# Gate and up of the FFN by seven half-size products for 19 of 22 feature tiles (Strassen's scheme) in a one-core DiT step

## The reference

```
def swiglu(h, wg, wu, wd):
    return (jax.nn.silu(h @ wg) * (h @ wu)) @ wd

xs = xs + gt2 * swiglu(modulate(rmsnorm(xs, g_ffn), sh2, sc2), w_gate, w_up, w_down)   # latent
xp = xp + ...                                                                          # context, the same
```

## Time and profile before

| | us |
|---|---|
| median of 3 runs | 970.76 (970.47, 970.76, 974.79) |
| the profiled execution | 974.25 |
| its span, first to last instruction | 972.3 |
| TensorE busy | 952.2 |
| VectorE busy | 492.9 |
| ScalarE busy | 356.7 |

### The profile page before, as it was taken

One profiled execution on the slowest core, in us unless ns is written; L12 is line 12 of the kernel. 1 busy time (PEld: TensorE's weight loads), 2 busy tenths in 40 slices (PEclk: granted clock), 3 DMA queues, 4 the chain that ended last, 5 costly groups with the idle time before them and its releaser, 6 DMA issues.

```text
span 972.3 us, 16382 instructions
## 1 busy us (share of the span) xinstructions
PE 952.2 (98%) x6613; PEld 894.5 (92%) x6613; DVE 492.9 (51%) x898; ACT 356.7 (37%) x675; POOL 2.8 (0%) x8
## 2 busy tenths in 40 slices
PE   5999999999999999999999999999999999999998
PEld 5688888778878999999999999999999999999998
DVE  4557898798788553233476233242323323333332
ACT  4563454667766422222257232211222221122220
POOL 0000000000000000000000000000000000000000
PEclk7899999999999999999999999999999999999999
DMA  9745333532353122422122212122222213122221
GB/s 373 297 176 185 138 109 131 178 111 88 125 162 128 63 68 80 181 71 72 53 68 86 87 65 85 45 97 78 67 84 65 86 44 109 65 85 67 68 81 68
DMA packets 33066, 104.23 MB, mean 107 GB/s; under 512 B 3696, under 2 KB 8944, under 8 KB 31856
## 3 DMA queue, kind: packets, MB, share of 16 engines
q1 hardware_dynamic: 32288, 102.64, 30.6%
q10 hardware_dynamic: 720, 0.77, 0.2%
HBM read 99.07 MB, written 4.33 MB: 106 GB/s over the span
## 4 chain that ended last, share of the span: by engine, by line
PE 91%; DVE 4%; DMA 1%; ACT 1%; SPq 1%; issue 1%; ACTq 0%; DVEq 0%
PE ps L1280 65%; PE ps L1376 13%; PE ps L1584 4%; PE ps L1502 3%; PE ps L1476 2%; PE ps L1487 2%; PE ps L1329 1%; PE ps L1400 1%; DMA x<-w_ada 1%; DVE scr L922 1%; DMA vec<-vecs 1%; SPq L466 1%; ACT scr L547 0%; DVE scr L1073 0%; DVE w_lo L886 0%
## 5 line engine op out<-in xcount | busy, mean ns | idle before, releaser
L535 ACT ACTIVATE w_hi<-stage 128x1024 fp32r<-128x1024 f32 x118 | 124.5, 1060 | 312.1 <-PE ps L1280 269.3
L886 DVE TENSOR_TENSOR w_lo<-stage,w_hi 128x1024 fp32r<-128x1024 f32 x118 | 144.4, 1224 | 173.7 <-ACT w_hi L535 170.7
L1280 PE MATMUL ps<-h_hi,w_hi 128*128 128x320 f32 x896 | 208.5, 314 | 0.7 <-ACT scr L709 0.4
L1280 PE MATMUL ps<-h_lo,w_hi 128*128 128x320 f32 x896 | 204.1, 309 | 0.0
L1280 PE MATMUL ps<-h_hi,w_lo 128*128 128x320 f32 x896 | 204.0, 309 | 0.0
L1280 PEld LDWEIGHTS ps<-h_hi,w_hi 128*128 128x128 f32 x896 | 148.2, 188 | 10.9 <-issue 9.0
L1280 PEld LDWEIGHTS ps<-h_lo,w_hi 128*128 128x128 f32 x896 | 149.8, 188 | 0.0
L1280 PEld LDWEIGHTS ps<-h_hi,w_lo 128*128 128x128 f32 x896 | 149.8, 188 | 0.0
L1280 PE MATMUL ps<-y_hi,w_hi 128*128 128x320 f32 x480 | 109.4, 309 | 0.0
L1280 PE MATMUL ps<-y_hi,w_lo 128*128 128x320 f32 x480 | 109.3, 309 | 0.0
L1280 PE MATMUL ps<-y_lo,w_hi 128*128 128x320 f32 x480 | 109.3, 309 | 0.0
(11 more groups left out here) (166 smaller groups left out, 1162.6 us busy)
## 6 DMA issues: line engine op xcount, KB each, us to landing
stage<-w_main SPq DMA_DIRECT2D x118, 512.0 KB, 3.5
x<-w_ada SPq DMA_DIRECT2D x23, 512.0 KB, 4.7
qk<-w_ada SPq DMA_DIRECT2D x7, 1024.0 KB, 11.7
bb<-rpb SPq DMA_DIRECT2D x16, 256.0 KB, 4.4
qk<-w_ada SPq DMA_DIRECT2D x5, 512.0 KB, 3.9
x<-x_t SPq DMA_DIRECT2D x1, 2560.0 KB, 11.0
y_t<-x SPq DMA_DIRECT2D x8, 320.0 KB, 2.2
vf<-w_ada SPq DMA_DIRECT2D x4, 512.0 KB, 3.9
```

The costliest lines, as they stand in the source:

```text
L535: act.activation(w_hi[:, slot, :], stage[:, slot, :], ACT.Copy).then_inc(hi_done, 1)
L886: dve.tensor_tensor(w_lo[:, slot, :], stage[:, slot, :], w_hi[:, slot, :].bitcast(F32), ALU.subtract).then_inc(lo_done, 1)
L1280: ins = pe.matmul(out[:, half, :], wt[:, w_slot, w], rt[:, rk, half * TH:(half + 1) * TH], start=start and n == 0, stop=stop and n == 2)
```

## The change

The diff, cut to its core (semaphores, aliases and the calls of the head left out):

```diff
+N_STD = 3
+LEFT = ("A11", "A12", "S2", "S1", "S3", "S4", "A22")
+LEFT_AT = {"A11": (0, 0), "A12": (0, 512), "S2": (1, 0), "S1": (1, 512), "S3": (2, 0), "S4": (2, 512), "A22": (3, 0)}
+BANK_OF = {"A11": 0, "A12": 1, "S2": 2, "S1": 3, "S3": 4, "A22": 5, "S4": 6}
...
+        def unit_used(u):
+            for part, nf in enumerate(FF_PARTS):
+                for n in range(KT):
+                    if u == down_unit(part, n):
+                        return lo_done, split_number(part, n) + 1
+                for f in range(max(FF_FIRST[part], N_STD), FF_FIRST[part] + nf):
+                    if u == gate_unit(f):
+                        return left_lo["S4"], f - N_STD + 1
+                    if u == gate_unit(f) + 1:
+                        return left_lo["A22"], f - N_STD + 1
+            return lo_done, u + 1
...
+            for u in range(U_WO, N_UNITS):
+                sp.wait_ge(*unit_used(u - RING))
+                load_unit(u, u % RING)
...
+                for f in range(max(FF_FIRST[part], N_STD), FF_FIRST[part] + nf):     # ScalarE
+                    g, more = f - N_STD, f + 1 < FF_FIRST[part] + nf
+                    prev = f > max(FF_FIRST[part], N_STD)
+                    left_high("A22", g)
+                    if prev:
+                        half_tanh(g - 1, 1)
+                    copy_p1(g)
+                    if more:
+                        left_high("A11", g + 1)
+                    else:
+                        split_down(part, 0)
+                    if prev or f == N_STD:
+                        a_high(f - 1)
+                    if more:
+                        left_high("A12", g + 1)
+                    half_tanh(g, 0)
+                    if more:
+                        for op in ("S1", "S2", "S3", "S4"):
+                            left_high(op, g + 1)
+                    else:
+                        split_down(part, 1)
+                        half_tanh(g, 1)
+                        a_high(f)
...
+            def c11_u2(g):                                                            # VectorE
+                dve.wait_ge(left_used["S2"], g + 1)
+                dve.wait_ge(p1_copied, g + 1)
+                dve.tensor_tensor(two(H_C11, H_U2), of_product("A12", "S2"),
+                                  by_half[:, H_P1:H_P1 + 1, :].to_broadcast([P, 2, TH]), ALU.add).then_inc(c11_done, 1)
...
+                    if prev:
+                        c21_c12(g - 1)
+                    elif f == N_STD:
+                        gated_up(f - 1)
+                    left_low("A22", g)
+                    if prev:
+                        products_gated(g - 1)
+                    if more:
+                        left_low("A11", g + 1)
+                        s3(g + 1)
+                    else:
+                        down_low(part, 0)
+                    if prev or f == N_STD:
+                        a_low(f - 1)
+                    c11_u2(g)
+                    if more:
+                        left_low("A12", g + 1)
+                        s1(g + 1)
+                    v_sum(g)
+                    if more:
+                        s2(g + 1)
+                        s4(g + 1)
+                    else:
+                        down_low(part, 1)
+                    c22_u3(g)
+                    if more:
+                        for op in ("S1", "S2", "S3", "S4"):
+                            left_low(op, g + 1)
+                    else:
+                        c21_c12(g)
+                        products_gated(g)
+                        a_low(f)
...
+            def product(op, g):                                                       # TensorE
+                pe.wait_ge(left_lo[op], g + 1)
+                if g == 0 and op not in ("A11", "A12", "S4"):
+                    pe.wait_ge(t_ready, ("S1", "S2", "S3", "A22").index(op) + 1)
+                slot, at = LEFT_AT[op]
+                for k in range(4):
+                    w = slice(at + k * P, at + (k + 1) * P)
+                    for n, (wt, part) in enumerate(((w_hi, 0), (w_hi, 1), (w_lo, 0))):
+                        ins = pe.matmul(ps[:, BANK_OF[op], 0:TH], wt[:, slot, w], right(op, part, k),
+                                        start=k == 0 and n == 0, stop=k == 3 and n == 2)
+                ins.then_inc(left_used[op], 1)
...
+                        free = [(p1_copied, g), (c11_done, g), (v_done, g), (c22_done, g), (c12_done, g)]
+                    pe.wait_ge(*free[0])
+                    product("A11", g)
+                    pe.wait_ge(*free[1])
+                    product("A12", g)
+                    product("S2", g)
+                    pe.wait_ge(*free[2])
+                    product("S1", g)
+                    pe.wait_ge(*free[3])
+                    product("S3", g)
+                    pe.wait_ge(*free[4])
+                    product("S4", g)
+                    product("A22", g)
```

More of the change, by code:

```diff
@@ new lines, in gate_tanh, with a_high, t_high @@
+            def gate_tanh(f):
+                act.wait_ge(pe_unit, U_FFN + 2 * f + 1)
+                act.activation(halves(ft[f % 2]), slot_ps(2 * (f % 2)), ACT.Tanh, scale=0.5).then_inc(tanh_done, 1)
+            def a_high(f):
+                act.wait_ge(a32_done, f + 1)
+                part = sum(f >= first for first in FF_FIRST) - 1
+                act.activation(y_hi[:, f - FF_FIRST[part], :], fp[f % 2], ACT.Copy).then_inc(ahi_done, 1)
+            def t_high(i):
+                act.wait_ge(t_sum, i + 1)
+                full = (t1_sb[:, :, :], t2_sb[:, :, :], b1[:, :, TH:T], b2[:, :, 0:TH])[i]
+                act.activation(t_hi[:, 4 * i:4 * i + 4, :], full, ACT.Copy).then_inc(t_hi_done, 1)
@@ new lines, in split_down @@
+            def split_down(part, n):
+                u = down_unit(part, n)
+                last = FF_FIRST[part] + FF_PARTS[part] - N_STD
+                act.wait_ge(*unit_arrived(u))
+                if n < 4:
+                    act.wait_ge(left_used[("A12", "S1", "S4", "A22")[n]], last)
+                else:
+                    act.wait_ge(pe_unit, split_number(part, n - 4) + 1)
+                act.activation(w_hi[:, n % 4, :], stage[:, u % RING, :], ACT.Copy).then_inc(hi_done, 1)
+            gate_tanh(0)
@@ new lines, in down_low @@
+            def down_low(part, n):
+                number = split_number(part, n)
+                dve.wait_ge(hi_done, number + 1)
+                slot = n % 4
+                dve.tensor_tensor(w_lo[:, slot, :], stage[:, down_unit(part, n) % RING, :], w_hi[:, slot, :].bitcast(F32),
+                                  ALU.subtract).then_inc(lo_done, 1)
+            t_sums(0)
+            gated(0)
+            split_lo(U_FFN + 4, (U_FFN + 4) % RING)
+            gated_up(0)
+            split_lo(U_FFN + 5, (U_FFN + 5) % RING)
@@ L1613, in _ @@
                         rms2_stats(1)
-            for part, nf in enumerate(FF_PARTS):
[L1615 to L1630, removed]
+            for m in range(2):
+                pe.wait_ge(lo_done, U_FFN + 4 + m + 1)
+                if m == 0:
+                    pe.wait_ge(a32_done, 1)
+                unit(m, (U_FFN + 4 + m) % RING, h_hi, h_lo).then_inc(pe_unit, 1)
@@ L1648, in _tiles @@
+                    unit(n % 4, n % 4, y_hi, y_lo, nk=nf).then_inc(pe_unit, 1)
 def _tiles(w):
```

303 lines of the change are left out of this document (231 added, 72 removed).

## The result

The changed kernel took 939.03 us (median of 4 runs, 937.37 to 939.53) against 970.81 (4 runs) for the kernel before; the ratio is 0.9664, 95% interval 0.9649 to 0.9679. It is faster, by 31.8 us on these medians; the forecast was 937.3 us and 33.4.

What follows compares the result with a forecast made beforehand. TensorE, busy 98% of the span, was taken as the bound by its matmul count; 228 fewer at 0.14664 us take 33.4 us off the 970.76 us median, giving 937.3 us. Range 934.5 to 945.5 us.

Steps and rivals of the forecast that it cites:

- The removed matmuls: FFN on TensorE: 228 matmuls fewer over 19 tiles at 0.14664 us each, 33.4 us less if TensorE never waits.
- VectorE's round: VectorE's work for one FFN tile, summed start to start: 11.8 us, fitting into TensorE's 12.32 us.
- rival A: FFN rounds: VectorE becomes the bound, each instruction taking its whole duration; round 13.1 us, total 941 us; chance 0.13.
- The free lag: FFN rounds: work made about a round ahead, so VectorE may lag 4.7 us in each part without cost.
- a part's end: Last round before the down units: low halves ready 2.3 us early, 1.5 us of idle VectorE in front; no cost.
- the rule of 4.7: FFN parts: VectorE's lag costs time only beyond 4.7 us, the slack before product S2's low half is needed.
- The head: Before the first product: gated(2) is ready 1.7 us before TensorE needs it, so TensorE stays gapless.
- ScalarE, DMA, straight code: FFN rounds: ScalarE about 5.6 us, no bound; weight loads in time; straight code at the same pace as loops.
- The sum: Whole kernel: median 970.76 us less 33.4 us gives 937.3 us.
- Rivals A to D: Besides rival A: slower product pace, 943 us, 0.07; open bank handovers, 1003, 0.03; head or part-end stalls, 943, 0.07.

Runs made afterwards that it cites:

- b_84: Kernel before with 12 of 96 matmuls left out in each of the 20 FFN tiles its loop runs, nothing else moved; 936.10 us.
- a_96: Changed kernel with an eighth product in each of the 19 tiles, repeating the last one into an unused bank; 972.06 us.
- a_v1: Changed kernel with one more VectorE addition of 640 elements in each of the 19 rounds; 937.83 us.
- a_v3: Changed kernel with three more VectorE additions of 640 elements in each of the 19 rounds; 958.27 us.
- a_v2: Changed kernel with two more VectorE additions of 640 elements in each of the 19 rounds; 941.78 us.
- b_straight: Kernel before with the hardware loops of the FFN and of SP's weight loads written out as straight code; 972.04 us.
- b_again: Kernel before, unchanged, run again for a second profile; 971.02 us.
- a_again: Changed kernel, unchanged, run again for more runs beside the kernel before on the same chip; 936.80 us.
- a_head: Changed kernel with five more dependent VectorE additions of 640 elements in its head, before the first gating; 941.55 us.

## Why the prediction was right

**The removed matmuls.** 228 x 0.14664, in one piece of 403 us at 0.1467: as forecast. b_84 shows it without the rest of the change, a_96 the rest of the change without it.

**VectorE's round.** Forecast 11.8 us in 12.32. Measured, a_v1 to a_v3 less 0.71 to 0.74 for each extra instruction: 11.7. The sizes 0.82, 0.69 and 0.49 and the overlap of 0.09 held for the new forms; too large was the price of the first gating before the second, 0.11 for two waits: they start 702.11 - 701.25 = 0.86 apart, the 0.03 of one wait. The second wait there was long fulfilled. Whole durations one behind the other (rival A) would have put L1443 0.68 behind L1435; it came 0.60 behind (702.85, 703.45). The Trainium skill's sentence that the next operation does not start until the pipe is empty (VectorE: DVE Perf Modes, "The DRAIN you can't avoid") is not borne out by this row, but the same paragraph adds that an operation that is not held starts earlier, and with that the row agrees. The prediction quotes the first without the second; read whole, the section does not demand rival A's round.

**The free lag.** It was argued, and the change alone does not need it, as its round is shorter than TensorE's. a_v1 shows that a VectorE round 0.12 above TensorE's costs nothing, a_v2 and a_v3 that some 4 to 4.7 us are free: lag less loss is 3.9, 4.1 and 4.1 us in the three parts of a_v2, and 4.7 to 4.8 in those of a_v3. The prediction's own numbers for a part's end, 2.3 us to spare and 1.5 idle in front, together 3.8, were nearer to a_v2 than the 4.7 that it took from S2. The part ends, which I priced at nothing for the change, are free for the change (no stop in its chain) but are the second place to stop once VectorE lags. Rival A did price them, at up to 2 us: its sum of 3.8 for a round of 13.1 is near the 4.1 measured in a_v2 at 13.17, where the rule of 4.7 alone gives 2.5.

**The head.** gated(2) started at 542.44 in the changed kernel, done at 543.3, 1.7 us before the first product at 544.96: the forecast's distance to a tenth.

**ScalarE, DMA, straight code.** TensorE has no stop in the changed kernel's FFN, so none is theirs; b_straight shows the third by itself. ScalarE's work in a round of part two is about 6.2 us, where 5.6 was forecast, without consequence beside 12.32.

**The sum.** 937.3 against 939.03 first and 936.80 later. The first median misses by 1.7 us. In the profiled executions that is the start of the kernel and not a term of the sum: b_again took 971.07 and begins its piece at 528.87, the changed kernel begins it at 530.88, and 971.07 - 33.4 + 2.0 = 939.7, against 939.53 measured. For the other runs of the median, which have no profile, it is inferred. The scatter of the start was known only as the spread of three runs, and the two medians fall on both sides of 937.3, by 1.7 and 0.5 us. Rivals A to D did not occur: the round is 12.32, the pace 0.1467, and there is no stop.

## What to carry to other kernels

Where one engine runs without a stop for hundreds of microseconds, a scheme that trades its instructions for another engine's work is priced by their number times its spacing. The other side of the trade is one question: does the second engine's round, summed start to start and not by busy time, fit into the first one's? If work is made a round ahead, even a longer round is free until the lag over the whole stage passes the distance between making and using. Look for the shortest such distance at the end of the stage too (here the down pairs), and count the rounds until something resets the lag. An opened handover cost 1.19 us in each round here, more than the 0.82 of the work waited for, so order the waits for the latest possible use.

## What the runs showed of the hardware that was not expected

The granted clock fell once in the middle of the kernel in three of the twelve profiles. In a_again and a_head it was in the last h tiles before the FFN, where TensorE waits 0.2 to 0.4 us for VectorE between groups of three matmuls; in a_v3 it was at the start of the last down units, 1.6 us behind a wait of 1.9 us (shown above). In a_again the window and the matmuls (start us, us):

```profile
518.00:530.00 12.00, 12.00 (x72) 12.00 (x73) 10.64 (x10) 8.57 (x11) 0.00 (x0) 0.86 0.30 90
```

```profile
518.21 0.47 PE L1899 MATMUL ps<-h_lo,w_hi 128*128 128x320 f32 x1
518.48 0.47 PE L1899 MATMUL ps<-h_hi,w_lo 128*128 128x320 f32 x1
518.74 0.47 PE L1899 MATMUL ps<-h_hi,w_hi 128*128 128x320 f32 x1
...
521.74 0.31 PE L1899 MATMUL ps<-h_hi,w_hi 128*128 128x320 f32 x1
521.88 0.30 PE L1899 MATMUL ps<-h_lo,w_hi 128*128 128x320 f32 x1
```

They start 0.267 us apart, 320 columns at 1.2 GHz, until 521.4 and then 0.147 apart; the stretch of 75 took 12.80 us in place of 11.26. At the lower level the spacing is just the 320 columns (320 / 1.2 = 267 ns); at 2.4 GHz it is 147 ns where the columns alone would be 133. The Trainium skill (TensorE: Matmul & The Clock Gate, "Back-to-back issue gap") gives N / 1.2 at the lower level, with which this agrees, and N / 2.4 + 2.5 ns, 136, at the upper, where the rows have 147; it gives the formula for isolated matmuls and says that it does not hold for a stream with weight loads, which this is.

What makes the clock fall in some executions and not in others is open. In a_v3 the same wait of 1.9 us stands in front of the down units of parts one and two as well (at 612.14 and 774.69), and there the clock stayed at 1.00; a_v1 has the same groups of three in front of its FFN and no fall.
